# One activation-table set for logarithm and exponential, a later state load, and a new order of the prompt's attention products in a decoder trunk

## The reference, cut to what matters

```
x += RMSNorm_post(mixer(RMSNorm_pre(x)))
x += RMSNorm_post(MLP(RMSNorm_pre(x)))      # MLP = relu(h W_up)^2 W_down
```

```
q, k, v, r, gd = split(h @ w_in)
log_a = log_sigmoid(gd @ w_gate + b_gate) / 16
q_in, k_in, k_dec = q*exp(b), k*exp(-b), k*exp(b_last - b)
A = causal(q_in @ k_in.T)                   # attention products
o = A @ v + q_in @ s
s = exp(b_last) * s + k_dec.T @ v           # next chunk's state
o = rmsnorm(o) * silu(r);  mixer = o @ w_o
```

## Time and profile before

| what | us |
|---|---|
| median of three runs | 1509.04 (1508.36 to 1510.45) |
| the profiled execution's own time | 1513.13 |
| its span, first to last instruction | 1511.5 |
| PE busy | 1426.2 (94% of the span) |
| DVE, ACT, POOL busy | 695.6, 507.1, 306.8 |
| mean granted clock of PE | 0.978 of full |

### The profile page before, as it was taken

How to read it: one execution, slowest core, us unless ns; L and a number is a source line. 1 busy time by engine, 2 the same in 40 slices (tenths; PEclk the granted TensorE clock), 3 DMA queues, 4 the chain that set the end, 5 groups by cost and what they waited for, 6 DMA issues and landing times.

```text
span 1511.5 us, 28963 instructions
## 1 busy us (share of the span) xinstructions
PE 1426.2 (94%) x11605; PEld 1300.7 (86%) x11605; DVE 695.6 (46%) x1128; ACT 507.1 (34%) x965; POOL 306.8 (20%) x268
## 2 busy tenths in 40 slices
PE   7988998799999999999998999999989999999997
PEld 7655556679899999999997787889879999999996
DVE  4456765534733433434346545535453343343434
ACT  5345543233521212212235233433462121221223
POOL 2210003201330512404301000001033051240530
PEclk9999997999999999999999999999989999999998
DMA  8400003222232222232323233222223322332321
GB/s 238 117 7 1 1 16 104 74 85 70 58 96 85 84 84 83 83 84 83 97 57 115 60 102 100 86 86 76 67 55 94 89 84 85 89 90 83 85 70 60
DMA packets 203905, 120.27 MB, mean 80 GB/s; under 512 B 13990, under 2 KB 199616, under 8 KB 203808
## 3 DMA queue, kind: packets, MB, share of 16 engines
q1 hardware_dynamic: 197776, 104.74, 24.4%
q0 software_dynamic: 6032, 14.17, 3.0%
HBM read 111.30 MB, written 7.59 MB: 79 GB/s over the span
## 4 chain that ended last, share of the span: by engine, by line
PE 86%; DVE 7%; ACT 4%; issue 2%; DMA 1%; SPq 0%; DVEq 0%; ACTq 0%
PE ps L1864 60%; PE ps L1927 6%; PE ps L2084 2%; PE ps L2120 1%; PE ps L2178 1%; PE ps L2243 1%; ACT w_hi L819 1%; DVE stat L1473 1%; PE ps L2103 1%; DVE w_lo L1292 1%; PE ps L1888 1%; PE ps L2261 1%; DVE y L1320 1%; DVE qT L1465 1%; DVE x L1327 1%
## 5 line engine op out<-in xcount | busy, mean ns | idle before, releaser
L819 ACT CAST w_hi<-w_raw 128x1024 fp32r<-128x1024 f32 x172 | 180.2, 1049 | 687.1 <-PE ps L1864 662.8
L1864 PE MATMUL ps<-act_hi,w_hi 128*128 128x280 f32 (+1 forms) x1408 | 299.3, 294 | 9.0 <-DVE relu L1612 5.2
L1864 PE MATMUL ps<-act_hi,w_lo 128*128 128x280 f32 (+1 forms) x1408 | 296.7, 292 | 0.0
L1864 PE MATMUL ps<-act_lo,w_hi 128*128 128x280 f32 (+1 forms) x1408 | 296.0, 292 | 0.0
L1292 DVE TENSOR_TENSOR w_lo<-w_raw,w_hi 128x1024 fp32r<-128x1024 f32 x172 | 254.3, 1480 | 76.6 <-ACT w_hi L819 76.6
L1864 PEld LDWEIGHTS ps<-act_hi,w_hi 128*128 128x128 f32 x1408 | 224.9, 190 | 15.5 <-issue 14.3
L1864 PEld LDWEIGHTS ps<-act_hi,w_lo 128*128 128x128 f32 x1408 | 225.5, 190 | 0.0
L1864 PEld LDWEIGHTS ps<-act_lo,w_hi 128*128 128x128 f32 x1408 | 224.8, 190 | 0.0
L1864 PE MATMUL ps<-h_hi,w_lo 128*128 128x280 f32 (+1 forms) x928 | 193.6, 290 | 0.0
L1864 PE MATMUL ps<-h_hi,w_hi 128*128 128x280 f32 (+1 forms) x928 | 192.9, 289 | 0.0
L1864 PE MATMUL ps<-h_lo,w_hi 128*128 128x280 f32 (+1 forms) x928 | 192.8, 289 | 0.0
(11 more groups left out here) (328 smaller groups left out, 1927.1 us busy)
## 6 DMA issues: line engine op xcount, KB each, us to landing
w_raw<-in_mlp_w_up_dram SPq DMA_DIRECT2D x64, 512.0 KB, 4.1
w_raw<-in_mlp_w_down_dram SPq DMA_DIRECT2D x64, 512.0 KB, 3.9
w_raw<-in_gla_w_in_dram SPq DMA_DIRECT2D x24, 512.0 KB, 3.8
pg_ckv<-in_cache_ckv_dram SPq DMA_DIRECT2D x64, 128.0 KB, 2.5
w_raw<-in_mla_w_o_dram SPq DMA_DIRECT2D x8, 512.0 KB, 4.3
sts<-in_state_gla_dram POOLq DMA_DIRECT2D x4, 1024.0 KB, 6.2
out_dram<-sts POOLq DMA_DIRECT2D x4, 1024.0 KB, 5.1
w_raw<-in_gla_w_o_dram SPq DMA_DIRECT2D x8, 512.0 KB, 4.0
```

What stands on the lines that cost most here:

```text
L819: nc.scalar.copy(w_hi[slot(g)][:], w_raw[raw_slot(g)][:]).then_inc(w_rounded, 1)
L1864: last = nc.tensor.matmul(out[:, h, 0:n], w[:, c, :], a[:, c, t0 + n * h:t0 + n * h + n], start=(c == 0 and k == 0), stop=(c == DC - 1 and ...
```

## The change

1. On POOL, the first two state loads each get a wait ahead of them on `w_split`: the load for head 0 until the fourth of layer 1's input blocks is split, the load for head 1 until the eighth is.
2. On ACT, the set `natural_log_exp_and_others` is loaded by name behind the eighth and last `gate_silu`.
3. On PE, in `scores(h)`, the four attention products of the prompt come first, and the wait for `kd_tok` and the meta product that reads it come behind them.

```diff
             nc.gpsimd.memset(kdpad[:], 0.0).then_inc(pads_zeroed, 1)
+            pool.wait_ge(w_split, G_GLA_IN + 4)
             load_states(0)
+            pool.wait_ge(w_split, G_GLA_IN + 8)
             load_states(1)
...
             gate_silu(7)
+            nc.scalar.preload_act_table_set("natural_log_exp_and_others")
             round_gated(7)
...
-                pe.wait_ge(turn_read, TURN_OF[f"KD{h}"] + 1)
-                nc.tensor.matmul(ps[:, 7, GV:2 * GV], kd_tok[0:META, 0, :], v[0:META, 0, :], start=True, stop=True)
                 for i in range(1, NT):
                     t0 = TILES[i][0]
                     nc.tensor.matmul(ps[:, 6, P * (i - 1):P * i], gk[:, t0:t0 + P], gq[h % 2][:, t0:t0 + P], start=True, stop=True)
+                pe.wait_ge(turn_read, TURN_OF[f"KD{h}"] + 1)
+                nc.tensor.matmul(ps[:, 7, GV:2 * GV], kd_tok[0:META, 0, :], v[0:META, 0, :], start=True, stop=True)
```

## The result

| | before | changed |
|---|---|---|
| time of the launch, us | 1508.7 (4 runs, 1507.1 to 1510.45) | 1496.0 (4 runs, 1494.83 to 1499.01) |
| changed / before | | 0.9902, 95% interval 0.988 to 0.9924 |
| profiled execution: own time, span | 1513.13, 1511.5 | 1496.14, 1494.5 |
| mean granted clock of PE | 0.978 | 0.988 |
| PE, ACT busy | 1426.2, 507.1 | 1416.7, 493.1 |

The change made the kernel faster by 12.7 us between the medians, which is 0.84%. The ratio on record, 0.9902, is not the quotient of these two medians (0.9916); it stands for 14.8 us. PE was busy for 9.5 us less with the same 11605 matmuls, beside a mean clock that rose from 0.978 to 0.988; I put that part down to the clock. ACT lost 14.0 us of work, eleven loads.

What follows compares the result with a forecast made beforehand. PE holds 86% of the chain, so time is won where it waits or runs slowly. 5.3 + 3.9 + 4.0 + 0.3 = 13.5 us off 1513.13 gives 1499.6, less 4.1 carried over 1495.5 us; range 1491.5 to 1500.5.

Steps and rivals of the forecast that it cites:

- loads on the chain: Boundary 2's inverse roots and the end: table loads the chain goes through disappear; 5.3 us, bounds 5.1 to 6.4.
- clock: Boundary 2 and the end: shorter PE idles leave fewer half-clock stretches behind them; 3.9 us, between 0 and 6.0.
- scores: Four heads: attention products fill PE's wait for `kd_tok`; 4 x 1.0 = 4.0 us, bounds 0 and 4.3.
- states: Layer 1's mixer entry: later load 1 stops sharing DMA with the chain's weight block; 0.3 us, bounds -0.2 and +0.6.
- 0.15, 1.28 and 1.28: Exposed load time at boundary 2's first-half post norm, its second-half pre norm, and the end, in us.
- pass while PE works: Boundary 2, pre norm: the first half's two loads lie beside PE's work; only 1.28 us of the second half's counts.
- The rival that ACT stands still beside each load: Each of four exposed loads costs about its length again; another 5.1 us, giving 1490.4; chance 0.02.
- The 54 products: Matmuls behind boundary 2's wait for `act_lo`: 9.66 us becomes 7.7 at full clock; 1.9 us back, bounds 0 and 2.1.
- The term behind the boundary: MLP behind boundary 2's `relu` wait: idle shrinks from 3.2 to 1.9 us, clock returns 1.6 us, bounds 0 and 3.2.
- the fourth rival's first half: PE keeps full clock to boundary 2's end, another 1.6 us; whole rival gives 1493.3, chance 0.04.
- 1.28 + 0.4: The end: one exposed table load, 1.28 us, plus 0.4 from the last transposes' clock, where DVE's x sets the pace.
- The rival that the next wait takes the gain back: Heads: PE then waits on DVE's states or ACT's copies, the 4.0 us is lost, giving 1499.5; chance 0.08.

Runs made afterwards that it cites:

- `loads_exposed`: The changed kernel with the four table loads found on the chain put back; 1507.09 us, 0.9962 of before.
- `loads_hidden`: The changed kernel with the eight table loads found beside other work put back; 1499.9 us, 0.9906 of before.
- `scores_only`: The kernel before with only the new order of the scores on PE; 1507.19 us, 0.995 of before.
- `states_only`: The kernel before with only the two waits on POOL ahead of the state loads; 1512.49 us, 0.9994 of before.
- `before_filled`: The kernel before, all loads in place, with throwaway products in three PE idles (two of boundary 2, one at the end); 1508.26 us, 0.9975 of before.
- `tables_only`: The kernel before with only the table set loaded by name behind the last gate; 1504.04 us, 0.9936 of before.
- the filled kernel: The changed kernel with throwaway products in PE's longer idles of the boundaries, mixer entry and end; two series: 1496.64 us (0.9899 of before) and 1496.31 us (0.9888).
- `after_third`: The changed kernel itself, run again beside the filled one in a third series; 1498.97 us, 0.9906 of before.
- `states_later`: The changed kernel with the first two state loads moved to the eighth and ninth input block's split; 1497.0 us (one run).

## Why the prediction was right, point by point

The forecast of 1495.5 us was right, and so were its mechanisms for the loads, the clock and the scores; that of the states is too small to be told in time. Its sizes against the stages:

| term | predicted | measured between the two profiles |
|---|---|---|
| loads on the chain | 5.3 | 5.4 |
| clock | 3.9 | 4.8 |
| scores | 4.0 | 3.7 |
| states | 0.3 | 0.1 |
| not told by a term | 0 | 0.2 |
| sum | 13.5 | 14.2 |
| by which the profile of before stood above its median, carried over | 4.1 | 2.8 in the attention |

**The loads.** Right, by place and by size, for this profile of before. The second half's products came 2.7 us earlier against the sum ahead of them, for 2.57. The rest of the 5.4 is taken as forecast, 0.15, 1.28 and 1.28: the chain of `loads_exposed` has its loads back at 1.28 each, and `loads_hidden` has 0.1 for the first step. The eight others were worth 1.1 us in `loads_hidden`, and one part of the reasoning fails there: that the pre norm's first loads "pass while PE works" held only for a PE as slow as in before's profile, and not in those of `scores_only`, `states_only` and `before_filled`. So the terms for loads and for clock are not independent, and I had added them as if they were. It cost nothing here, since the change removed these loads too.

**A switch costs its load.** The rival that ACT stands still beside each load, about as long again, is refuted: 0.03 us lie beside the load of `loads_exposed`, and the stage at the end, with one load on the chain, fell by 1.7 us and not by 2.6 or more. The Trainium skill, ScalarE: Activation LUTs, section What ACT_TABLE_LOAD costs, gives 1283 ns for the load, which the trace agrees with to the nanosecond, and some 1380 ns of drain besides, which no run here shows.

**The clock.** Right in kind, and `before_filled` shows the cause by itself: with all loads in place, full clock behind the three idles gave 3.8 us against before's profile and 1.9 against two others. The 54 products gained 1.84 us, for 1.9. The term behind the boundary was mis-sized: I took 1.6, and 3.8 - 1.28 = 2.5 came. My model was layer 0, where a wait of 2.0 us has a slow stretch behind it. The changed kernel's wait had the same length, but no stretch behind it; these are its waits of PE (us in total, times, longest) from 1020 to 1122, and its granted clock behind the first and the second of the boundary's idles and at the end:

```profile
PE ps L1867 <- DVE relu L1615: 2.0, 1, 2.0
PE ps L1930 <- DVE act_lo L1336: 1.3, 2, 1.1
```

```profile
1094.00:1100.00 6.00, 5.33 (x37) 4.92 (x38) 5.86 (x15) 4.13 (x11) 0.00 (x0) 1.00 0.27 80
1108.00:1116.00 8.00, 7.15 (x57) 7.18 (x58) 5.04 (x6) 4.09 (x6) 7.12 (x5) 1.00 0.40 113
1483.00:1488.00 5.00, 3.45 (x20) 1.80 (x21) 5.00 (x14) 0.80 (x2) 0.00 (x0) 1.00 0.52 210
```

In three profiles of the changed kernel this stage was 371.1 each time, in `tables_only`, with the same instructions and the same wait there, 372.6. So behind 2.0 us of idle the clock fell in some profiles and not in others, and 1.6 was one of two outcomes; this is the fourth rival's first half. The size depends on before's execution as much: loads and clock together were forecast at 9.2 us, and from boundary 2 to the end the changed kernel is 10.2 us shorter than before, but 8.2 and 8.4 shorter than `scores_only` and `states_only`. At the end 1.7 came for 1.28 + 0.4, and DVE's x sets it, as I had said: PE waits 0.22 us for it ahead of the last transposes, with nothing left of its own to do.

```profile
1487.30 0.80 DVE L1330 TENSOR_TENSOR x<-x,y 128x272 f32<-128x272 f32 x2
...
1487.80 0.90 PE L2491 MATMUL ps<-cst,x 128*128 128x128 f32 x6 [0.22 <-DVE x L1330]
```

**The scores.** Right. The four attention products (8 rows) run while ACT copies `kd_tok`, and the meta product starts when that ends, here ahead of the second head's scores:

```profile
880.95 1.06 PE L2381 MATMUL ps<-gq,gla_tmp 128*128 128x128 f32 x8
881.15 0.91 ACT L1143 COPY kd_tok<-ps 128x896 f32<-128x896 f32 x1
...
882.11 0.69 PE L2383 MATMUL ps<-gv,kd_tok 16*128 16x256 f32 x2
```

3.7 us came for 4.0, in `scores_only` as in the whole. The rival that the next wait takes the gain back is refuted: in the changed kernel too the wait for `gv` is 1.7 us in 3 waits, as in `scores_only`.

**The states.** Load 1 went out at 828.97, for 831.7, in a kernel that reaches load 0 3.0 us sooner than before did, and nobody waits for it:

```profile
808.43 0.92 POOL L785 DMA_DIRECT2D sts<-in_state_gla_dram  x1
828.97 0.89 POOL L785 DMA_DIRECT2D sts<-in_state_gla_dram  x1 [19.61 <-DVE w_lo L1295]
```

The weight block on the chain landed in 4.38, 4.12, 4.07 and 4.32 us in the four profiles with both loads early (before, `tables_only`, `scores_only`, `before_filled`). It landed in 4.30, 3.91, 4.04, 3.88, 3.87, 3.79, 3.85 and 3.96 in the eight with load 1 late (the changed kernel three times, `states_only`, `loads_hidden`, `loads_exposed`, the filled kernel twice). The means are 4.22 and 3.95: 0.27 us for the 0.3 that I took, though the changed kernel alone spreads over 0.4, and the pair of profiles in the table has 0.1 of it. In time nothing can be told. The added table load had its cover: ACT idled 5.79 us behind it and one rounding, for 6.23 before.

```profile
1031.54 1.28 ACT L1267 ACT_TABLE_LOAD   x1
1032.83 0.65 ACT L1250 CAST o_hi<-og 128x544 fp32r<-128x544 f32 x1
1039.27 1.05 ACT L821 CAST w_hi<-w_raw 128x1024 fp32r<-128x1024 f32 x1 [5.79 <-PE ps L1891]
```

**The step that failed** is the carrying over. The profiled execution stood 4.1 us above the median of three runs, and I took that as a fixed offset to both kernels. It was one execution's clock: before's attention took 2.8 us longer than the changed kernel's, with a stretch at half clock that the other did not have, and the changed kernel's profiled execution stood only 0.1 us above its own median. So the profiled time fell by 14.2 + 2.8 = 17.0 us, from 1513.13 to 1496.14, where I had 1499.6. And the first runs of before were on the low side: over 55 later ones its mean was 1513.2. The gain by ratio was 0.94 to 1.02% in every series, 14 to 15 us, where I had 13.5. Between the two profiles what was short is the clock behind boundary 2. That the forecast fell within 0.5 us of 1496.0 is in part luck: the gain was taken too small, and the median that it was taken from was low.

## What to carry to other kernels

Count a load, a wait or a copy by its place on the chain, not by its number: of twelve loads four and a bit were worth something, and one new order of four products as much as three of them. Price an idle of PE with the clock behind it, but only where PE sets the pace there; filling it with throwaway products tells the two apart. When PE gets faster, ask again what was hidden behind it: three loads that cost nothing before would have cost 1.0 us afterwards. And take the sizes from more than one profile: before and `states_only`, with the same code behind their heads, were 1.9 us apart from boundary 2 on.

## What the runs showed of the hardware

- A kernel's spread from run to run goes with PE's mean granted clock. Over 55 runs of before, 0.001 of mean clock went with 0.86 us (correlation -0.89), from 1506.5 us at 0.985 to 1521.41 at 0.969. The same instructions had a stretch at half clock in one profile and none in another (236 to 244 us, clock 0.57 and 1.00). The stage that holds the attention varied most, between 348.5 and 354.7 us over thirteen profiles.
- A stretch at half clock cost 1.4 to 1.8 us where PE was the bound (48 products 7.79 for 6.43 us, 54 products 9.66 for 7.82), and 0.1 us or less in boundary 1 (461.7 us with one, 461.6 with none). The entry's first product group took 2.84 and 3.47 us for 2.13 where such a stretch fell on it (`after_third`, `states_later`).
- A table load cost its own 1283 ns where ACT's next instruction was waited for. Of the pre norm's four loads in boundary 2 all were on the chain with PE's idles filled and its clock full (`before_filled`), and one in before.
- With two state loads of 1 MB issued some 8 us ahead of it, a 512 KB weight block landed in 4.22 us on average of four profiles; with one, in 3.95 of eight; in the one profile with none, in 3.82. The first two groups overlap (4.07 to 4.38 and 3.79 to 4.30).
- Behind a wait of 2.0 us in layer 0 PE's clock fell in one profile of the changed kernel (0.79 over 8 us) and stayed full in another; behind 3.8 us it fell in before, and with the idle filled it did not.
